# Eighty-odd unread matmuls behind the last sums of a transformer layer

## The reference

```
def reference(x, ...):
    x = mixer_layer(x, ...)       # x + concat(attention A, attention B) @ w_out
    x = conv_ffn(x, ...)          # below
    return x

def conv_ffn(x, norm2_g, w_up, conv_w, conv_b, w_down):
    h = rms_norm(x, norm2_g)
    u = causal_depthwise_conv(h @ w_up, conv_w) + conv_b
    gate, val = split(u, 2)
    return x + (silu(gate) * val) @ w_down
```

## Time and profile before

| what | value |
|---|---|
| time, median of two runs | 1077.16 us (1077.05 to 1077.28) |
| time of the profiled execution | 1076.96 us |
| its span, first to last instruction | 1075.2 us |
| outside the span | 1.76 us |
| PE busy | 1063.5 us, 99% of the span |
| DVE, ACT, POOL busy | 758.9, 627.7, 105.3 us |

### The profile page before, as it was taken

One profiled execution on the slowest core, in us unless ns is written; L12 is line 12 of the kernel. 1 busy time (PEld: TensorE's weight loads), 2 busy tenths in 40 slices (PEclk: granted clock), 3 DMA queues, 4 the chain that ended last, 5 costly groups with the idle time before them and its releaser, 6 DMA issues.

```text
span 1075.2 us, 20163 instructions
## 1 busy us (share of the span) xinstructions
PE 1063.5 (99%) x6503; PEld 994.6 (93%) x6503; DVE 758.9 (71%) x1274; ACT 627.7 (58%) x1047; POOL 105.3 (10%) x125
## 2 busy tenths in 40 slices
PE   9999899999999999999999999999999999999998
PEld 8999899999998999999999999999999999999997
DVE  6767677767676778778778777878778744464444
ACT  6777577665655556666666666666666533434332
POOL 0101100000001113111111111111111100000000
PEclk9999899999999999999999999999999999999999
DMA  9744465656575766656666656666666666556664
GB/s 314 279 147 148 133 216 163 188 165 191 161 235 162 228 198 192 203 195 210 196 198 202 204 196 196 206 198 201 201 204 197 198 201 205 197 185 209 205 201 137
DMA packets 66764, 211.37 MB, mean 197 GB/s; under 512 B 9384, under 2 KB 11568, under 8 KB 66352
## 3 DMA queue, kind: packets, MB, share of 16 engines
q1 hardware_dynamic: 66736, 211.01, 61.3%
HBM read 208.88 MB, written 2.11 MB: 196 GB/s over the span
## 4 chain that ended last, share of the span: by engine, by line
PE 89%; DVE 4%; DMA 3%; ACT 3%; issue 1%; SPq 0%; DVEq 0%; ACTq 0%
PE ps L282 46%; PE ps L283 23%; PE ps L275 6%; PE ps L277 6%; PE ps L276 6%; DVE w_lo L838 2%; DMA raw<-in_w 1%; DMA raw<-in_win 1%; ACT w_hi L536 1%; PE ps L300 1%; ACT s_sb L584 1%; PE ps L292 1%; PE ps L299 0%; DVE xT L1267 0%; PE ps L309 0%
## 5 line engine op out<-in xcount | busy, mean ns | idle before, releaser
L838 DVE TENSOR_TENSOR w_lo<-raw,w_hi 128x1024 fp32r<-128x1024 f32 (+2 forms) x418 | 494.8, 1190 | 235.0 <-ACT w_hi L536 234.1
L536 ACT ACTIVATE w_hi<-raw 128x1024 fp32r<-128x1024 f32 (+2 forms) x418 | 413.2, 992 | 337.4 <-PE ps L283 272.4
L282 PE MATMUL ps<-xs,w_hi 128*128 128x512 f32 x1376 | 451.0, 382 | 0.0
L283 PE MATMUL ps<-xs,w_lo 128*128 128x256 f32 x1376 | 375.1, 273 | 0.0
L282 PEld LDWEIGHTS ps<-xs,w_hi 128*128 128x128 f32 x1376 | 260.1, 189 | 36.2
L283 PEld LDWEIGHTS ps<-xs,w_lo 128*128 128x128 f32 x1376 | 264.2, 192 | 0.0
L282 PE MATMUL ps<-a_s,w_hi 128*128 (+1 forms) x688 | 225.6, 382 | 0.1
L283 PE MATMUL ps<-a_s,w_lo 128*128 (+1 forms) x688 | 187.5, 273 | 0.0
L275 PE MATMUL ps<-w_hi,xs 128*128 128x384 f32 (+1 forms) x512 | 175.0, 342 | 3.3 <-DVE cT L1054 3.3
L276 PE MATMUL ps<-w_lo,xs 128*128 128x384 f32 (+1 forms) x512 | 168.0, 328 | 0.0
L277 PE MATMUL ps<-w_hi,xs 128*128 128x384 f32 (+1 forms) x512 | 168.0, 328 | 0.0
(11 more groups left out here) (153 smaller groups left out, 684.0 us busy)
## 6 DMA issues: line engine op xcount, KB each, us to landing
raw<-in_wrest SPq DMA_DIRECT2D x290, 512.0 KB, 4.2
raw<-in_win SPq DMA_DIRECT2D x120, 384.0 KB, 3.6
raw<-in_w SPq DMA_DIRECT2D x8, 392.0 KB, 5.4
xT<-in_xT SPq DMA_DIRECT2D x8, 256.0 KB, 5.4
xtok<-in_xtok SPq DMA_DIRECT2D x2, 1024.0 KB, 7.6
out<-xT SPq DMA_DIRECT2D x16, 128.0 KB, 2.3
cbc<-c_scratch SPq DMA_DIRECT2D x1, 1024.0 KB, 5.3
const<-in_const SPq DMA_DIRECT2D x1, 576.0 KB, 8.6
```

Of the source, the lines that this page charges most:

```text
L282: pe.matmul(bank(b), slot(w_hi, s, P, t * P), weave(acts), start=start, stop=False, skip_group_check=True)
L283: return pe.matmul(bank(b, S, S), slot(w_lo, s, P, t * P), part(acts, 0).rearrange("p k j -> p j k"), start=False, stop=stop, skip_group_c ...
L536: act.activation(slot(w_hi, s, w), slot(raw, s, w), ACT.Copy).then_inc(hi_ready, 1)
L838: dve.tensor_tensor(slot(w_lo, s, w), slot(raw, s, w), f32(slot(w_hi, s, w)), ALU.subtract).then_inc(split_done, 1)
```

## The change

After last_two(84, 0), PE waits until all 16 output tiles are summed (o_done), and then issues matmuls that read the old activations xs and the last weight pieces in w_hi and write to banks 0 and 1, which nobody reads any more. The helper probe(n, rhs) issues n matmuls with one moving operand and two stationary ones in turn.

```
--- before.py
+++ after.py
@@ -524,6 +524,38 @@
                 for b in range(4):
                     down_piece(j * 4 + b, j * 4 + (b - FT), b)
             last_two(84, 0)
+
+
+            pe.wait_ge(o_done, KT)
+            x0 = xs[:, 0:2 * S]
+
+            def probe(n, rhs, lhs=None, b=0):
+                lhs = [slot(w_hi, 0, P, i * P) for i in range(2)] if lhs is None else lhs
+                cols = int(np.prod(rhs.shape[1:]))
+                for i in range(n):
+                    pe.matmul(bank(b, 0, cols), lhs[i % 2], rhs, start=True, stop=True, skip_group_check=True)
+
+            def blocks(ap, w, k=2):
+                return ap.rearrange("p (k b i) -> p b k i", k=k, i=w)
+
+            for rhs in [x0, weave(x0)] + [blocks(x0, w) for w in (2, 4, 8, 16, 32, 64)]:
+                probe(4, rhs)
+            probe(4, x0.rearrange("p (o k b) -> p o b k", o=2, k=2))
+            probe(4, x0.rearrange("p (b k) -> p k b", k=2))
+            for gap in (260, 264, 272, 288, 512):
+                probe(4, xs[:, 0:2 * gap].rearrange("p (k b) -> p b k", k=2)[:, 0:S, :])
+            for i in range(3):
+                probe(1, weave(x0), b=1)
+                probe(1, weave(xs[:, 0:S]), b=1)
+            probe(4, weave(xs[:, 0:S]))
+            probe(4, xs[:, 0:P])
+            probe(4, weave(xs[:, 0:P]))
+            odd = [slot(w_hi, 0, 2 * P).rearrange("p (b k) -> p k b", k=2)[:, i] for i in range(2)]
+            probe(4, weave(xs[:, 0:P]), odd)
+            probe(4, weave(xs[:, 0:S]), odd)
+            probe(4, weave(x0), odd)
+            same = [slot(w_hi, 0, P)] * 2
+            probe(4, weave(xs[:, 0:S]), same)
```

## The result

The changed kernel takes 1093.91 us (two runs, 1093.86 and 1093.96) where the kernel before took 1077.16. The ratio is 1.0158 with an interval of 1.0134 to 1.0183: slower by 1.6%, less than the 2% taken as the least difference that counts. The forecast was 1094.8.

What follows compares the result with a forecast made beforehand. PE bounds the kernel, busy 99% of the span, so added matmuls cost their pitch: 7.63 + 8.80 + 1.64 + 1.31 = 19.4 us behind the last sum, span end 1093.0, time 1094.8 us, range 1092.0 to 1100.8.

Steps and rivals of the forecast that it cites:

- The start and the tail: Behind DVE's last sum: probes start at 1072.96, 0.06 after it, lose 0.10 at once; cover counts from 1072.90.
- 94, not 80: The probe list: the change's words say 80, the diff has 94 matmuls, and unread ones run all the same.
- 35 woven ones of 512 columns: Probes alternating between two streams, at any distance: 0.218 each, 7.63 us in all.
- The 32 in other orders: Probes of 512 columns in plain order, blocks or every second element: 0.275 each, 8.80 us, bounds 6.98 and 13.8.
- the four-way row: Warm-up matmuls woven from four quarters: 0.275 each, 1.26 times the woven pitch, taken as price for the 32.
- 27 narrow ones: Probes: 15 of 256 columns at 0.109, 1.64 us, and 12 of 128 at 0.109, 1.31 us.
- Sum and end: Probe list to span end: 19.4 us of pitches, 0.16 for the last matmul, 0.35 for the engines; end at 1093.0.
- Full rate for every order: Rival on the 32: they cost only 6.98 us, time 1092.9; chance 0.24.
- Half rate for plain order and blocks: Rival on the 32: plain order and longer blocks at 0.43, 13.8 us, time 1099.7; chance 0.27 with cases near it.
- The fall of the clock in the 1.2 us pause: Rival: PE's pause before the probes lowers its clock; 1097, or 1108.5 if it lasts to their end; chance 0.04.
- The float32 rows: Plain-order float32 matmuls in the trace: 0.86 ns a column, twice the woven price; order or type as cause left open.
- The sentence on lines: On the skill's rule of two accesses per 16-byte line: woven order changes line every access yet runs at 0.218.

Runs made afterwards that it cites:

- the run with the early start: Against the changed kernel, the probes wait for ten of the 16 last sums instead of all; 1092.3 us, ratio 1.0145.
- the all-woven list: Against the changed kernel, the same 94 matmuls by width, all in woven order; 1093.05 us, ratio 1.0148.
- the run on types and widths: Against the changed kernel's list, groups of 8 with float32 operands, fewer columns, or stationary operands read in steps; plain float32 of 256 columns took 0.216 a pass.

## Why the prediction was right

It was right in sign, size and range, and by its own steps except one: the single price of 0.275 for the 32 matmuls in other orders. Its parts were off both ways and cancelled, and that is luck.

- **The start and the tail**: the list was to begin 0.06 behind the last sum and lose 0.10 at once; it began 0.05 behind it, and the first pitch was 0.34 where plain order has 0.23, which is 0.11 lost. The pause counts in full, as the run with the early start showed.
- **94, not 80**: all were in the trace.
- **35 woven ones of 512 columns**: forecast 7.63 us at 0.218, measured 7.59. For two streams no distance that was run from 128 to 1024 elements, odd or even, costs anything.
- **The 32 in other orders**: forecast 8.80 us at 0.275. Measured 8.99 with the first pitch's 0.11, 8.88 without. The sum is right and the step was not: one price for all was taken from the four-way row. Plain order and blocks of 8 and more cost 0.23 to 0.245 (20 matmuls, 4.84 us with the first pitch's 0.11, where 5.5 was forecast), blocks of 4 0.253, blocks of 2 0.337 and every second element 0.447 (8 matmuls, 3.14 us where 2.2 was forecast). The two errors cancel by the make-up of this list: 32 matmuls in plain order alone would take 7.4 us, 32 with every second element 14.4 (estimates, 32 times 0.231 and 0.45). The prediction named plain order or blocks far from 0.275 as a sign that it was wrong, and by that sign this step failed. The row itself was read rightly: four streams 128 elements apart have 0.28 in a run of their own. What it could not do is stand for orders that it doesn't resemble.
- **27 narrow ones**: forecast 2.94 us, measured 3.06: 1.75 for those of 256 columns, where the four with a step of 2 in the weights add 0.09, and 1.31 for those of 128, as forecast. That a floor near 0.11 holds for the narrow ones was confirmed down to 32 columns.
- **Sum and end**: with the first pitch's surcharge 19.5 forecast, 19.63 measured; from the last matmul's end 0.24 instead of 0.35. Together the piece behind the last sum was forecast at 20.1 us (1072.90 to 1093.0) and was 20.09.
- **The 0.8 us that remain** between 1094.8 and 1093.96 lie before the list: the last sum ended at 1072.09 where the earlier trace rows has 1072.90. Before, PE worked at half clock from 118.4 to 123.3, 5 us, which costs 2.5; here it was 3.4 us (120.0 to 123.4), which costs 1.7. The difference is the 0.8. Matmul by matmul the changed kernel lies 0.14 us behind the kernel before at 117 us and 0.64 ahead of it at 124 us, the two sides of the fall. Such a shift is common to all kernels here and is no effect of the change.

**The rivals.** Full rate for every order: out, since the all-woven list takes 2.1 us less than the list of the change. Half rate for plain order and blocks: excluded for these, true only for every second element (0.45). The argument that I gave against it, that the four-way order alternates too and is slow, did point the right way. The fall of the clock in the 1.2 us pause: it stayed at 1.00 in the last 20 us. The float32 rows, which I could not tell apart, are slow by their type. One rival stands untested: every probe has a weight load beside it, so no run shows what the orders cost without one.

**The sentence on lines.** I wrote that the trace speaks against the rule of the Trainium skill (Advanced Engine Details and Errata, SBUF Cachelines) that two accesses in a row must hit a 16-byte line, because the woven order changes the line at each access. Read for one stream of accesses this is so. Read for two readers that take the elements in turn it fits the simpler orders (a hit is a read from the line that the reader is in): woven order gives each reader four hits a line (0.216), plain order two (0.23), steps of 2 and more one (0.45), two streams with a step of 2 two (0.229), with a step of 4 one (0.45). In float32, at half the rate, nearly the same numbers come back for half the columns, as if one reader did the work: 0.216 in plain order (four hits), 0.227 in steps of 2 (two hits), 0.273 woven (two streams for one reader, as four streams are for two, 0.28). The prices are shown; the two readers are a picture that orders most of them, not something a trace displays. By it four streams and blocks of 2 ask for a new line at every read, as a step of 2 does, yet they cost 0.28 and 0.33 and not 0.45. Nor does it explain why eight streams cost 0.49, more than a new line at every read, nor what distances do to four streams and to blocks of 4. So the mechanism stays open.

## What to carry to other kernels

Price a matmul by its pitch in the order in which it reads, and in its own type: for float32r weave two streams if the layout allows it (plain order cost this kernel 57.6 us, 5%), leave float32 in plain order, and keep off steps of two elements and more in a float32r moving operand and of four in a stationary one. Where several cases of unlike kind share one price in a forecast, a right sum proves none of them; ask for a run that changes the mix. When small effects are measured behind a long kernel, count from a mark close to them instead of comparing whole times.

## What the runs showed that was not expected

- Woven float32 is 26% slower than plain float32 (0.273 against 0.216 for 256 columns a pass), the opposite of float32r (0.216 against 0.230 for 512).
- A stationary operand read with a step of 4 elements takes 0.233 a matmul with 64 and with 256 columns and 0.236 with 512, more than a woven matmul of 512 columns itself; with a step of 2 it takes 0.118 and hides behind 512 columns (0.216), but not behind 256 (0.122 for 0.112).
- In the run on types and widths the granted clock was 0.51 from 1103.2 to 1106.7 us, after 10 us of matmuls of 32 to 256 columns without a pause between them; PE was busy all the time by its rows. The groups L587 and L589, 256 columns beside plain weights and weights with a step of 2, both ran at 0.213 there, so they say nothing of their prices. The two windows:

```profile
1093.32:1101.38 8.06, 8.06 (x75) 8.06 (x73) 0.00 (x0) 0.00 (x0) 0.00 (x0) 1.00 0.00 0
...
1103.24:1106.70 3.46, 3.46 (x17) 3.46 (x18) 0.00 (x0) 0.00 (x0) 0.00 (x0) 0.51 0.00 0
```
